# Two more tiles of each feed-forward stage by seven block products, and three of the four token sums on GpSimd, in a one-core macaron decoder layer

## The chip, the core and the metric

One Trainium2 chip, of which one core works. The metric is the device time of one execution of the whole layer in microseconds (us); three runs of the kernel before gave 2166.7, 2168.15 and 2168.75.

## What is computed

```python
x = x + 0.5 * _swiglu(_rmsnorm(x, ffn1_norm[l]), ffn1_w_gu[l], ffn1_w_down[l])
...
x = x + merged @ w_out[l]
x = x + 0.5 * _swiglu(_rmsnorm(x, ffn2_norm[l]), ffn2_w_gu[l], ffn2_w_down[l])

def _swiglu(h, w_gu, w_down):
    a, b = jnp.split(h @ w_gu, 2, axis=-1)
    return (jax.nn.silu(a) * b) @ w_down
```

1024 tokens, model width 1024, hidden width 2816, everything in float32. Between the two feed-forward stages stands a token-mixing block with three kinds of attention, which the change leaves alone. Each float32 product is made on TensorE from rounded parts: an operand is split into `hi` (rounded) and `lo` (the rest), and `hi*hi`, `hi*lo` and `lo*hi` are added up, so one product of blocks is three matmuls, and each operand needs an `hi` (made by ScalarE) and a `lo` (made by VectorE).

## The kernel before

**Layout.** Tokens lie transposed: `xT` holds 8 tiles of 128 model channels by 1024 tokens. The hidden width is 22 tiles of 128. A hidden tile needs a gate product and an up product (each 128 hidden by 1024 tokens, over 8 tiles of channels), then `silu(gate) * up / 2`, and two such tiles at a time (a group) are multiplied by their part of `w_down` and added to `xT`.

**Three ways to make a hidden tile.** Tiles 0 and 1 are made straight from `h = x * gain` (`h_hi`, `h_lo`), and scaled afterwards by the norm of each token (`rB`, in `ffn_gate`, `ffn_up`, lines 1427 to 1435). Each of these four products is a *unit* of 48 matmuls of 128x512. Tiles 2 and 3 (`by_halves`) are made with normed tokens instead, and are also 4 units of 48. From tile 4 on (`PLAIN = 4`) gate and up of one tile are made together as a product of 2x2 blocks by *seven* block products instead of eight; each block product is a *part* of 12 matmuls (`seventh`), so a tile is 84 matmuls instead of 96. From group 2 on the down product too is made by seven parts (`pair`).

**Normed tokens.** The seven products need the four quadrants of the normed tokens (512 channels by 512 tokens, stored as 128x2048) and four sums or differences of them. `quadrant` (L1454) makes one by four VectorE instructions from `xT`, gain and `rB`; `tokens_sum` (L1473) makes a sum; `tokens_hi` (L938, ScalarE) and `tokens_lo` (L1462, VectorE) split each into `tok_hi` and `tok_lo`, 128x2048 each. The buffers lie on top of `h_hi`, `h_lo` and of scratch memory.

**The order around the change.** Every engine runs a list written by hand and waits on semaphores. TensorE: gate and up of tiles 0 and 1; then `ffn`: the first half of the gate of tile 2 (24 matmuls), `down_plain` (group 0: eight output tiles `m`, 96 matmuls, first both `m = 0, 1` for hidden tile 0, then for hidden tile 1), the rest of tiles 2 and 3, then the parts of tiles 4 to 21. In the first stage a small product for the attention bias (`toe`) stands just ahead of `ffn`, and `down_plain` waits until VectorE has copied it out of PSUM (`toe_kept`), since it uses the same banks. VectorE scales and splits tiles 0 and 1, makes quadrants and `tok_lo`, adds each finished down tile to `xT` (`add_tile`, L1488), which also sets PSUM free for TensorE, and makes the `lo` of each part's weights (`part_lo`, L1581). GpSimd adds up squares for the norm (`square_sums`, L783) and makes the sums of weight blocks that the parts need (`weights_sum`, L804 to L812), in the order of its list.

The line on which TensorE waits in `down_plain` before it can go on to the second hidden tile:

```python
pe.wait_ge(split_done, u + 3)
pe.wait_ge(a_ready, A_COUNT * f + 2)
for m in range(2):
    whole(m, 1).then_inc(down_done, 1)
for m in range(2, DT):
    pe.wait_ge(down_added, ADD_COUNT * f + m - 1)
```

`a_ready` counts the finished `a_lo` (L1448) of hidden tiles 0 and 1, `f` is the stage (0 or 1).

Of the kernel before, what the change touches and what calls it, by code (L numbers as in the profile page):

```python
# [48 lines left out]

PLAIN, SEVEN, NQ = 4, 7, 4  # L50
TILES7 = FT - PLAIN
FFN_UNITS = 10
# [11 lines left out]
U_HALVES = (U_SB - 6, UNITS - 6)  # L64
# [83 lines left out]


# [188 lines left out]
def layer(nc, x, mem, weights, gains, head_gains, rel_bias, consts, onehot, out):  # L338
    ctx = ExitStack()
    with ctx:  # L340
# [42 lines left out]
        oh = at("oh", AR + 56 * K, [33, TOE])  # L383
# [3 lines left out]
        toe = at("toe", AR + 62 * K, [2, TOE])  # L387
# [27 lines left out]
        raw2 = [at("raw2_0", RAW, [P, 2, 1024]), at("raw2_1", WH + 4 * K, [P, 2, 1024])]  # L415
        RING = (WH, WL, WL + 4 * K, WL + 8 * K)
# [89 lines left out]
        mem_in, ident_in, cst_in, gain_in, hgain_in = (sem(n) for n in ("mem_in", "ident_in", "cst_in", "gain_in", "hgain_in"))  # L506
# [49 lines left out]
        tok_made, tok_hi_done, tok_split, a_summed = (sem(n) for n in ("tok_made", "tok_hi_done", "tok_split", "a_summed"))  # L556
# [12 lines left out]
        TILE_COUNT, TOK_COUNT = a_count(FT - 1), 22  # L569
# [22 lines left out]
        def after_slot(eng, f, n):  # L592

            if n >= NQ:
                eng.wait_ge(part_done, NPART * f + n - NQ + 1)
            else:
                eng.wait_ge(unit_done, U_HALVES[f] + (4, 4, 5, 6)[n])

        def after_chunk(eng, f, c, *halves):

            for half in halves:
                if c % 2:
                    eng.wait_ge(chunk_in[half], 16 * (CHUNKS // 2 * f + c // 2 + 1))
                else:
                    eng.wait_ge(raw_in[half], 16 * ((U_HALVES[f] + 6) // 2 + CHUNKS // 2 * f + c // 2 + 1))
# [115 lines left out]
        def _(sp):  # L721
# [10 lines left out]
            sp.dma_start(hg_raw[:], head_gains).then_inc(hgain_in, 16)  # L732
# [41 lines left out]
        def _(pool):  # L774
# [104 lines left out]
            square_sums(2)  # L879
            weights_sums(1)  # L880
# [3 lines left out]
        def _(act):  # L884
            def split_hi(k):
# [4 lines left out]
                if k in (U_SB, U_SB + 1):  # L890
# [37 lines left out]
            def tokens_hi(f, i):  # L928

                if i < 4:  # L930
                    act.wait_ge(tok_made, TOK_COUNT * f + 4 * i + 4)
                else:
                    act.wait_ge(tok_made, TOK_COUNT * f + 18 + (1, 3, 2, 4)[i - 4])
                if i == 4 and f == 0:
                    act.wait_ge(toe_out, 16)
                if i >= 6:
                    act.wait_ge(unit_done, U_HALVES[f] + 6)
                nc.scalar.activation(tok_hi[i][:], tok[i][:], ACT.Copy).then_inc(tok_hi_done, 1)  # L938

# [63 lines left out]
            def behind_part(f, n):  # L1003
# [6 lines left out]
                if p == 0:  # L1010
                    if t < PLAIN + 2:
                        act.wait_ge(unit_done, U_HALVES[f] + 2)
# [3 lines left out]
                elif p == 1:  # L1016
                    if i % TILES7:
                        act.wait_ge(glu_done, (TILE_COUNT - 2) * f + a_count(t - 1) - 3)
# [9 lines left out]
                elif t == FT - 1:  # L1028
                    act.wait_ge(glu_done, (TILE_COUNT - 2) * f + a_count(t) - 3)
                    act.wait_ge(part_done, NPART * f + part_at("pair", ND, 5) + 1)  # L1030
                    nc.scalar.activation(a_hi[s][:, T1], a_full[s][:, T1], ACT.Copy).then_inc(a_hi_done, 1)
                    act.wait_ge(glu_done, (TILE_COUNT - 2) * f + a_count(t) - 2)
                    nc.scalar.activation(a_hi[s][:, T0], a_full[s][:, T0], ACT.Copy).then_inc(a_hi_done, 1)

            def ffn(f):

                u = U_HALVES[f]
                split_hi(u + 2)
                tokens_hi(f, 2)
# [1946 lines left out]
```

## Time and profile before

| what | value |
|---|---|
| median of 3 runs | 2168.15 us |
| the profiled execution's own time | 2167.03 us |
| its span, first to last instruction | 2165.1 us |
| TensorE busy | 2146.0 us, 99% |
| VectorE busy | 1584.1 us, 73% |
| ScalarE busy | 911.7 us, 42% |
| GpSimd busy | 468.8 us, 22% |
| granted clock of TensorE | 1.0 |

The span is what the trace covers; the execution's own time is 1.9 us longer. Matmuls are pipelined, so that the duration of one (0.39 us) is longer than the step from one start to the next. PE is TensorE, PEld its weight loads, DVE VectorE, ACT ScalarE, POOL GpSimd, SP SyncE. "Idle before" in a row is the time in which the engine did nothing before it, with what ended that time.

### The profile page before, as it was taken

To read this page: it belongs to the slowest core of one execution; us is meant where nothing else is said; L and a number is where in the kernel's file an instruction comes from. 1 tells how busy PE (TensorE), PEld (TensorE's weight loads), DVE (VectorE), ACT (ScalarE), POOL (GpSimd) and SP (SyncE) were. 2 spreads that over 40 slices of the span, in tenths; PEclk is the share of its full clock that TensorE was granted. 3 is DMA by queue.
4 is the path that set the end of the run, shared out by engine and by line. 5 is a ranking of instruction groups with operands and counts; after the bars stand their busy time and mean duration, and the time that the engine had idled before them with its cause. 6 is when DMAs were issued, how large, how long until landed. Compare 5 with 4: busy or idle time off the path is not lost.

```text
span 2165.1 us, 26379 instructions
## 1 busy us (share of the span) xinstructions
PE 2146.0 (99%) x9968; PEld 1733.8 (80%) x9968; DVE 1584.1 (73%) x1809; ACT 911.7 (42%) x1433; POOL 468.8 (22%) x396
## 2 busy tenths in 40 slices
PE   8999999999999999999999999999999999999999
PEld 7788888888887777777778888888888888888887
DVE  7978888888888788777536343355778888888885
ACT  6334333443445777846443111133333344343433
POOL 3013333323333122221000000002013332333330
PEclk9999999999999999999999999999999999999999
DMA  5211111111113200011112111131111111111113
GB/s 174 63 59 59 50 58 59 59 47 42 59 59 105 88 30 20 20 49 40 40 21 78 49 49 52 56 127 39 49 49 59 59 59 42 47 59 59 54 54 98
DMA packets 47630, 126.55 MB, mean 58 GB/s; under 512 B 4301, under 2 KB 20973, under 8 KB 47248
## 3 DMA queue, kind: packets, MB, share of 16 engines
q1 hardware_dynamic: 45600, 112.61, 16.2%
q10 hardware_dynamic: 912, 10.11, 1.3%
q0 software_dynamic: 992, 2.15, 0.5%
q8 instruction: 80, 1.31, 0.3%
q14 instruction: 46, 0.38, 0.1%
HBM read 116.42 MB, written 9.87 MB: 58 GB/s over the span
## 4 chain that ended last, share of the span: by engine, by line
PE 92%; DVE 5%; issue 1%; ACT 1%; DMA 0%; POOL 0%; SPq 0%; DVEq 0%; ACTq 0%
PE ps L2153 91%; DVE h_lo L1410 1%; DVE tok_lo L1462 1%; PE ps L2770 0%; DVE xT L1755 0%; DVE q_lo L1581 0%; PE ps L2705 0%; DVE h_lo L2065 0%; DVE xT L1488 0%; PE ps L2865 0%; DVE w_lo L1403 0%; DMA x_nat<-in_x 0%; ACT sb_l L1212 0%; POOL sb_l L829 0%; DVE a_lo L1534 0%
## 5 line engine op out<-in xcount | busy, mean ns | idle before, releaser
L2153 PE MATMUL ps<-tok_hi,q_hi 128*128 128x512 f32 x1008 | 392.7, 390 | 1.4 <-issue 1.0
L2153 PE MATMUL ps<-tok_lo,q_hi 128*128 128x512 f32 x1008 | 392.2, 389 | 0.0
L2153 PE MATMUL ps<-tok_hi,q_lo 128*128 128x512 f32 x1008 | 392.1, 389 | 0.0
L2153 PE MATMUL ps<-h_hi,w_hi 128*128 128x512 f32 x960 | 373.2, 399 | 1.7 <-ACT h_hi L1135 1.1
L2153 PE MATMUL ps<-h_lo,w_hi 128*128 128x512 f32 x960 | 363.9, 391 | 2.6 <-DVE h_lo L1410 2.1
L1547 DVE TENSOR_TENSOR xT<-xT,ps 128x1024 f32<-128x1024 f32 x252 | 302.8, 1218 | 60.2 <-PE ps L2153 49.0
L2153 PE MATMUL ps<-h_hi,w_lo 128*128 128x512 f32 x960 | 305.4, 390 | 0.0
L2153 PEld LDWEIGHTS ps<-tok_hi,q_hi 128*128 128x128 f32 x1008 | 189.2, 188 | 42.7 <-issue 2.4
L2153 PEld LDWEIGHTS ps<-h_hi,w_hi 128*128 128x128 f32 x960 | 179.9, 188 | 51.3 <-issue 15.7
L2153 PEld LDWEIGHTS ps<-tok_hi,q_lo 128*128 128x128 f32 x1008 | 189.2, 188 | 39.3
L2153 PEld LDWEIGHTS ps<-tok_lo,q_hi 128*128 128x128 f32 x1008 | 189.3, 188 | 38.9
L2153 PEld LDWEIGHTS ps<-h_hi,w_lo 128*128 128x128 f32 x960 | 180.3, 188 | 38.7
L2153 PEld LDWEIGHTS ps<-h_lo,w_hi 128*128 128x128 f32 x960 | 180.1, 188 | 38.2 <-DVE h_lo L1410 2.5
L2153 PE MATMUL ps<-b_hi,q_hi 128*128 128x512 f32 x504 | 196.1, 389 | 0.0
L2153 PE MATMUL ps<-b_hi,q_lo 128*128 128x512 f32 x504 | 196.1, 389 | 0.0
L804 POOL TENSOR_TENSOR q_sum<-raw 128x512 f32<-128x512 f32 x72 | 78.7, 1093 | 526.9 <-PE ps L2153 366.6
L1403 DVE TENSOR_TENSOR w_lo<-raw,w_hi 128x1024 fp32r<-128x1024 f32 x84 | 115.1, 1373 | 76.8 <-ACT w_hi L896 67.4
L783 POOL TENSOR_TENSOR acc<-acc,sq 128x1024 f32<-128x1024 f32 x21 | 53.9, 2566 | 405.1 <-ACT sq L903 404.9
L2153 PE MATMUL ps<-a_lo,q_hi 128*128 128x512 f32 x352 | 137.0, 389 | 0.0
L1001 ACT ACTIVATE q_hi<-q_sum 128x512 fp32r<-128x512 f32 x108 | 68.3, 632 | 142.0 <-POOL q_sum L810 58.2
L2005 DVE TENSOR_TENSOR gate<-ps,rB 128x1024 f32<-128x1024 f32 x24 | 29.4, 1225 | 129.8 <-PE ps L2153 129.8
L1581 DVE TENSOR_TENSOR q_lo<-raw,q_hi 128x512 fp32r<-128x512 f32 x144 | 124.0, 861 | 0.0
(309 smaller groups left out, 3706.6 us busy)
## 6 DMA issues: line engine op xcount, KB each, us to landing
raw<-in_weights SPq DMA_DIRECT2D x195, 512.0 KB, 3.6
x_keep<-xT ACTq DMA_DIRECT2D x1, 4096.0 KB, 12.4
x_back<-x_keep ACTq DMA_DIRECT2D x1, 4096.0 KB, 12.2
x_nat<-in_x SPq DMA_DIRECT2D x7, 512.0 KB, 7.3
out<-y_nat SPq DMA_DIRECT2D x7, 512.0 KB, 3.2
toe_keep<-toe_row ACTq DMA_DIRECT2D x2, 704.0 KB, 6.2
m_nat<-in_mem SPq DMA_DIRECT2D x1, 1024.0 KB, 7.9
d_fB<-d_f_keep POOLq DMA_DIRECT2D x2, 512.0 KB, 6.3
```

The source lines that it names most:

```text
L783: nc.gpsimd.tensor_tensor(acc[:], acc[:], sq[:, k % 2, :], ALU.add).then_inc(acc_done, 1)
L804: nc.gpsimd.tensor_tensor(to, a21, a22, ALU.add).then_inc(w_summed, 1)
L1001: nc.scalar.activation(q_hi[n % NQ][:], src, ACT.Copy).then_inc(part_hi_done, 1)
L1403: nc.vector.tensor_tensor(w_lo[:, w_slot(k)].rearrange("p a b -> p (a b)"), raw[:, k % NRAW, :], w_hi[:, w_slot(k)].rearrange("p a b -> p ...
L1410: nc.vector.scalar_tensor_tensor(out=h_lo[:, k, :], in0=xT[:, k, :], scalar=g32[:, gain, k:k + 1], in1=h_hi[:, k, :].bitcast(F32), op0=ALU ...
L1462: nc.vector.tensor_tensor(tok_lo[i][:], tok[i][:], tok_hi[i][:].bitcast(F32), ALU.subtract).then_inc(tok_split, 1)
L1547: nc.vector.tensor_tensor(to, to, ps[:, 2 + half, :].rearrange("p (a c) -> p a c", a=2), ALU.add).then_inc(down_added, 1)
L1581: nc.vector.tensor_tensor(q_lo[n % NQ][:], src, hi, ALU.subtract).then_inc(part_split, 1)
L2005: nc.vector.tensor_tensor(gate_tile(m, b), ps[:, merge_pair(m, b), :], rB[:], ALU.mult).then_inc(mg_taken, 1)
L2153: return pe.matmul(o, a, b, start=start, stop=stop, skip_group_check=True)
```

## The change

Tiles 2 and 3 are made by seven block products too (`PLAIN = 2`); `by_halves`, `halves_silu` and `halves_product` go. Only 7 versions of the tokens are kept, instead of 8. Of the four sums VectorE makes one (`tok[1]`), inside the new `first_tokens`, and GpSimd three, in the new `tokens_sums`. VectorE makes all four quadrants ahead of scaling tile 1's up product, and all seven `tok_lo` between the additions of group 0. ScalarE makes all seven `tok_hi` only after the last plain gate or up unit (`unit_done >= U_END - GT`). Group 0's down tiles go over all four PSUM pairs (`first_pair`) instead of two. The weight slots become `k % 3`. The head gains' arrival is counted with the constants', and at the end of the first stage the split of the next unit's weights stands one part later.

```diff
-PLAIN, SEVEN, NQ = 4, 7, 4
+PLAIN, SEVEN, NQ = 2, 7, 4
...
+def first_pair(m):
+
+    return (2, 3, 0, 1, 2, 3, 2, 3)[m]
...
+            def tokens_sums(f):
+
+                pool.wait_ge(tok_made, TOK_COUNT * f + 13)
+                nc.gpsimd.tensor_tensor(tok[4][:], tok[3][:], tok[4][:], ALU.subtract).then_inc(tok_summed, 1)
+                pool.wait_ge(unit_done, U_END[f] - GT)
+                nc.gpsimd.tensor_tensor(tok[2][:], tok[3][:], tok[1][:], ALU.subtract).then_inc(tok_summed, 1)
+                pool.wait_ge(tok_made, TOK_COUNT * f + 17)
+                pool.wait_ge(tok_summed, TOK_SUMS * f + 2)
+                nc.gpsimd.tensor_tensor(tok[6][:], tok[5][:], tok[2][:], ALU.subtract).then_inc(tok_summed, 1)
+
             square_sums(0)
+            tokens_sums(0)
             weights_sums(0)
...
             def tokens_hi(f, i):
 
-                if i < 4:
-                    act.wait_ge(tok_made, TOK_COUNT * f + 4 * i + 4)
+                act.wait_ge(unit_done, U_END[f] - GT)
+                if i in (2, 4, 6):
+                    act.wait_ge(tok_summed, TOK_SUMS * f + {4: 1, 2: 2, 6: 3}[i])
...
+            def first_tokens(f):
+
+                quadrant(f, 4, 0, 1)
+                tokens_sum(f, 1, 4, 0, 8)
+
+            def other_tokens(f):
+
+                quadrant(f, 3, 1, 1)
+                quadrant(f, 5, 1, 0)
...
-                quadrant(f, 2, 0, 1)
                 add_tile(f, 0, 0)
+                tokens_lo(f, 0)
                 add_tile(f, 0, 1)
-                quadrant(f, 3, 1, 1, 0, 2)
+                tokens_lo(f, 1)
                 add_tile(f, 0, 2)
-                quadrant(f, 3, 1, 1, 2, 4)
+                tokens_lo(f, 2)
+                part_lo(f, 0)
                 add_tile(f, 0, 3)
-                tokens_lo(f, 2)
-                add_tile(f, 0, 4)
                 tokens_lo(f, 3)
...
+                part_lo(f, 1)
+                for i in range(4, SEVEN):
+                    add_tile(f, 0, i)
+                    tokens_lo(f, i)
+                add_tile(f, 0, DT - 1)
...
                 for m in range(2, DT):
-                    pe.wait_ge(down_added, ADD_COUNT * f + m - 1)
+                    if m == 2:
+                        pe.wait_ge(gate_scaled, GT * (f + 1))
+                    elif m == 3:
+                        pe.wait_ge(up_scaled, PLAIN * (f + 1))
+                    else:
+                        pe.wait_ge(down_added, begin + (1, 2, 5, 6)[m - 4])
...
-                u = U_HALVES[f]
-                pe.wait_ge(split_done, u + 1)
-                pe.wait_ge(gate_scaled, 2 * f + 2)
-                by_halves(f, 0, u, 0)
                 down_plain(f)
-                by_halves(f, 0, u, 1).then_inc(unit_done, 1)
...
-                by_halves(f, 1, u + 5, 0)
-                by_halves(f, 1, u + 5, 1).then_inc(unit_done, 1)
                 for n in range(NPART):
                     pe.wait_ge(part_split, NPART * f + n + 1)
```

VectorE's list in the second feed-forward stage, around the end of tile 1's up product. Before (`tok_113` to `tok_120` are the eight token buffers in order, `a_up_80` the scaled up product of tile 1, `a_lo_76` the piece that TensorE waits for, L1488 the additions to `xT`):

```order
L1454 SCALAR_TENSOR_TENSOR tok_114<-xT,g_58,rB 128x512 x4
L1462 TENSOR_TENSOR tok_lo_106<-tok_114,tok_hi_98 128x2048
L1435 SCALAR_TENSOR_TENSOR a_up_80<-ps,rB 128x1024
L1442 TENSOR_TENSOR a_full_72<-a_up_80,a_full_72 128x1024
L1444 CAST a_hi_82<-a_full_72 128x1024
L1403 TENSOR_TENSOR w_lo<-raw,w_hi 128x1024
L1448 TENSOR_TENSOR a_lo_76<-a_full_72,a_hi_82 128x1024
L1454 SCALAR_TENSOR_TENSOR tok_115<-xT,g_58,rB 128x512 x4
L1488 TENSOR_TENSOR xT<-xT,ps 128x1024 x2
```

With the change (`tok_111` to `tok_117` are the seven buffers, `tok_104` and up their `lo`; L1446 is `quadrant`, L1461 `tokens_sum`, L1427 and L1434 to L1440 scale and split tile 1):

```order
L1446 SCALAR_TENSOR_TENSOR tok_115<-xT,g_58,rB 128x512 x4
L1461 TENSOR_TENSOR tok_112<-tok_115,tok_111 128x2048
L1422 TENSOR_TENSOR a_full_72<-ps,rB 128x1024
L1395 TENSOR_TENSOR w_lo<-raw,w_hi 128x1024
L1446 SCALAR_TENSOR_TENSOR tok_114<-xT,g_58,rB 128x512 x4
L1446 SCALAR_TENSOR_TENSOR tok_116<-xT,g_58,rB 128x512 x4
L1427 SCALAR_TENSOR_TENSOR a_up_80<-ps,rB 128x1024
L1434 TENSOR_TENSOR a_full_72<-a_up_80,a_full_72 128x1024
L1436 CAST a_hi_82<-a_full_72 128x1024
L1440 TENSOR_TENSOR a_lo_76<-a_full_72,a_hi_82 128x1024
```

Between the gate scaling (L1422) and the up scaling (L1427) of tile 1 stood one quadrant, and now two stand; a sum stands ahead of the gate scaling. The `tok_lo` and the `w_lo` of tile 2's weights are gone from this place.

What follows on VectorE with the change, from the first addition (L1486 is `add_tile`, L1456 `tokens_lo`, L1572 `part_lo`); the pattern goes on to the eighth addition:

```order
L1486 TENSOR_TENSOR xT<-xT,ps 128x1024
L1456 TENSOR_TENSOR tok_lo_104<-tok_111,tok_hi_97 128x2048
L1486 TENSOR_TENSOR xT<-xT,ps 128x1024
L1456 TENSOR_TENSOR tok_lo_105<-tok_112,tok_hi_98 128x2048
L1486 TENSOR_TENSOR xT<-xT,ps 128x1024
L1456 TENSOR_TENSOR tok_lo_106<-tok_113,tok_hi_99 128x2048
L1572 TENSOR_TENSOR q_lo_124<-raw_0_118,q_hi_120 128x512
L1486 TENSOR_TENSOR xT<-xT,ps 128x1024
L1456 TENSOR_TENSOR tok_lo_107<-tok_114,tok_hi_100 128x2048
L1572 TENSOR_TENSOR q_lo_125<-q_sum_129,q_hi_121 128x512
L1486 TENSOR_TENSOR xT<-xT,ps 128x1024
```

Before, two `tok_lo` and two quadrants stood between the eight additions; now it is seven `tok_lo` and two `part_lo`.

GpSimd's list with the change, where before the first weight sum (`q_sum<-raw`) followed directly on the sums of squares:

```order
L784 TENSOR_TENSOR acc<-acc,sq 128x1024 x7
L824 TENSOR_TENSOR tok_115<-tok_114,tok_115 128x2048
L826 TENSOR_TENSOR tok_113<-tok_114,tok_112 128x2048
L829 TENSOR_TENSOR tok_117<-tok_116,tok_113 128x2048
L805 TENSOR_TENSOR q_sum_129<-raw_0_118 128x512
L808 TENSOR_TENSOR raw_0_118<-q_sum_129,raw_0_118 128x512
```

Three instructions of 128x2048 have come in between, each with both inputs in SBUF.

## Rows read from the trace of the kernel before

**Rows 1.** Page, busy time of each engine, share of the span and instructions
```profile
PE 2146.0 (99%) x9968; PEld 1733.8 (80%) x9968; DVE 1584.1 (73%) x1809; ACT 911.7 (42%) x1433; POOL 468.8 (22%) x396
```
**Rows 2.** Waits of TensorE over the span: total us, times, longest us
```profile
PE ps L2153 <- DVE h_lo L1410: 2.1, 1, 2.1
PE ps L2153 <- issue: 1.0, 2, 0.5
PE ps L2153 <- DVE q_lo L1581: 0.4, 2, 0.2
```
**Rows 3.** Timeline, TensorE, second stage: start us, us, instruction, count
```profile
1549.88 0.39 PE L2153 MATMUL ps<-tok_hi,w_hi 128*128 128x512 f32 x1
...
1555.32 0.39 PE L2153 MATMUL ps<-a_hi,w_hi 128*128 128x512 f32 x1
...
1615.73 0.39 PE L2153 MATMUL ps<-tok_hi,q_hi 128*128 128x512 f32 x1
```
**Rows 4.** Timeline, VectorE, second stage, around the end of tile 1's up product
```profile
1540.04 1.22 DVE L1430 TENSOR_TENSOR a_full<-ps,rB 128x1024 f32<-128x1024 f32 x1
1543.33 1.23 DVE L1403 TENSOR_TENSOR w_lo<-raw,w_hi 128x1024 fp32r<-128x1024 f32 x1 [2.07 <-ACT w_hi L896]
1544.47 2.73 DVE L1454 SCALAR_TENSOR_TENSOR tok<-xT,g,rB 128x512 f32<-128x512 f32 x4
...
1551.40 1.22 DVE L1435 SCALAR_TENSOR_TENSOR a_up<-ps,rB 128x1024 f32<-128x1024 f32 x1
1552.72 1.23 DVE L1442 TENSOR_TENSOR a_full<-a_up,a_full 128x1024 f32<-128x1024 f32 x1
1553.98 0.69 DVE L1444 CAST a_hi<-a_full 128x1024 fp32r<-128x1024 f32 x1
...
1555.73 1.22 DVE L1448 TENSOR_TENSOR a_lo<-a_full,a_hi 128x1024 fp32r<-128x1024 f32 x1
```
**Rows 5.** Timelines of GpSimd and VectorE at 18 us and at 1508 us
```profile
18.70 2.39 POOL L783 TENSOR_TENSOR acc<-acc,sq 128x1024 f32<-128x1024 f32 x1 [1.07 <-ACT sq L903]
...
19.77 2.40 DVE L1410 SCALAR_TENSOR_TENSOR h_lo<-xT,g,h_hi 128x1024 fp32r<-128x1024 f32 x1
...
1507.68 5.81 DVE L1410 SCALAR_TENSOR_TENSOR h_lo<-xT,g,h_hi 128x1024 fp32r<-128x1024 f32 x3
...
1508.93 3.47 POOL L783 TENSOR_TENSOR acc<-acc,sq 128x1024 f32<-128x1024 f32 x1 [9.37 <-ACT sq L903]
```
**Rows 6.** Timelines of VectorE (input in PSUM) and GpSimd at 126 us
```profile
126.04 1.23 DVE L1504 SCALAR_TENSOR_TENSOR a_full<-ps,a_full 128x1024 f32<-128x1024 f32 x1 [0.80 <-PE ps L2153]
...
126.09 1.29 POOL L804 TENSOR_TENSOR q_sum<-raw 128x512 f32<-128x512 f32 x1 [85.47 <-PE ps L2153]
```
**Rows 7.** Groups by line: busy us, mean ns; and durations, min/median/max ns
```profile
L1488 DVE TENSOR_TENSOR xT<-xT,ps 128x1024 f32<-128x1024 f32 x31 | 37.8, 1218 | 21.3 <-PE ps L2153 20.6
L1462 DVE TENSOR_TENSOR tok_lo<-tok,tok_hi x16: 2282/2285/3380, 72.8 to 1624.3; 128x2048 fp32r<-128x2048 f32 x16
L938 ACT ACTIVATE tok_hi<-tok x16: 1898/1920/1922, 64.1 to 1620.9; 128x2048 fp32r<-128x2048 f32 x16
```
**Rows 8.** Timelines of VectorE and TensorE in the first stage
```profile
72.76 2.28 DVE L1462 TENSOR_TENSOR tok_lo<-tok,tok_hi 128x2048 fp32r<-128x2048 f32 x1
...
79.14 2.53 PE L2153 MATMUL ps<-oh,rel 33*2 33x256 f32 x10
...
83.02 1.20 DVE L1819 COPY toe<-ps 2x1024 f32<-2x1024 f32 x1
84.15 0.54 DVE L1820 COPY toe<-ps 2x384 f32<-2x384 f32 x1
...
137.28 0.68 DVE L1581 TENSOR_TENSOR q_lo<-raw,q_hi 128x512 fp32r<-128x512 f32 x1
```
**Rows 9.** Timeline, TensorE, opening: eight transposes after idle time, and later
```profile
9.85 1.91 PE L2477 MATMUL ps<-cst,x_nat 128*128 128x128 f32 x8
...
15.16 1.03 PE L2477 MATMUL ps<-cst,x_nat 128*128 128x128 f32 x8
```

More of the change, by code:

```diff
@@ L96 @@
     CHUNK += [("tile", _t)]
-    if _t % 2 == 1:
+    if _t % 2 == 1 and _t > 3:
         CHUNK += [("pair", (_t - 3) // 2)]
@@ L100 @@
         PARTS += [("tile", _t, _p, _c)]
-        if _t % 2 == 1:
+        if _t % 2 == 1 and _t > 3:
             PARTS += [("pair", (_t - 3) // 2, _p, _c + 1)]
@@ L1668, in ffn @@
                         pair_sums(f, (of - 2) // 2, p == 2)
-                    if kind == "tile" and of % 2 == 0 and p >= 2:
+                    if kind == "tile" and of % 2 == 0 and of > PLAIN and p >= 2:
                         pair_lo(f, (of - 2) // 2, p - 2)
-                    if kind == "tile" and of % 2 == 1 and p == 0:
+                    if kind == "tile" and of % 2 == 1 and of > PLAIN + 1 and p == 0:
                         pair_lo(f, (of - 3) // 2, 5)
@@ L1678, in ffn @@
                     if kind == "down":
-                        if f == 0 and n == NPART - 2:
+                        if f == 0 and n == NPART - 1:
                             split_lo(U_SB)
@@ L1800, in _ @@
             ffn_up(0, U_FIRST[0][1], 0)
-            quadrant(0, 0, 1, 0)
+            quadrant(0, 0, 0, 0)
             proj_final(1)
@@ L1811, in _ @@
             proj_final(3)
-            tokens_lo(0, 0)
+            first_tokens(0)
+            split_lo(9)
             dve.wait_ge(unit_done, U_MEM[3] + 1)
-            quadrant(0, 1, 0, 0)
-            split_lo(9)
-            tokens_lo(0, 1)
+            other_tokens(0)
             ffn_up(0, U_FIRST[1][1], 1)
@@ L2134, in _ @@
             ffn_gate(1, U_FFN2, 0)
+            quadrant(1, 0, 0, 0)
             split_lo(U_FFN2 + 3)
-            quadrant(1, 0, 1, 0)
             ffn_up(1, U_FFN2 + 1, 0)
@@ L2139, in _ @@
             split_lo(U_FFN2 + 4)
-            tokens_lo(1, 0)
+            first_tokens(1)
             ffn_gate(1, U_FFN2 + 2, 1)
             split_lo(U_FFN2 + 5)
-            quadrant(1, 1, 0, 0)
-            tokens_lo(1, 1)
+            other_tokens(1)
             ffn_up(1, U_FFN2 + 3, 1)
-            glu_product(1, 1, lambda: split_lo(U_FFN2 + 6))
+            glu_product(1, 1)
             ffn(1)
@@ L2226, in gate_or_up_part @@
                     last.then_inc(unit_done, 1)
-            def by_halves(f, part, k, half):
-                for half_d in (1, 0):
-                    i = ((1, 0), (2, 3))[half][half_d]
-                    pe.wait_ge(tok_split, 8 * f + i + 1)
-                    for j in range(4):
-                        hi, lo = (w[:, w_slot(k), 4 * half_d + j, :] for w in (w_hi, w_lo))
-                        mm(bank(2 * part + half), hi, tok_hi[i][:, j, :], half_d == 1 and j == 0, False)
-                        mm(bank(2 * part + half), hi, tok_lo[i][:, j, :], False, False)
-                        last = mm(bank(2 * part + half), lo, tok_hi[i][:, j, :], False, half_d == 0 and j == 3)
-                return last
             def seventh(f, n):
@@ L2258, in seventh @@
                     pe.wait_ge(seven_added, 3 * i + 2)
-                pe.wait_ge(tok_split, 8 * f + (5, 5, 6, 6, 7, 7, 8)[p])
+                pe.wait_ge(tok_split, SEVEN * f + p + 1)
                 for j in range(4):
                     hi, lo = (w[n % NQ][:, j * P:(j + 1) * P] for w in (q_hi, q_lo))
-                    mm(to, hi, tok_hi[of][:, j, :], j == 0 and p in (0, 1, 5), False)
-                    mm(to, hi, tok_lo[of][:, j, :], False, False)
-                    last = mm(to, lo, tok_hi[of][:, j, :], False, j == 3)
+                    mm(to, hi, tok_hi[p][:, j, :], j == 0 and p in (0, 1, 5), False)
+                    mm(to, hi, tok_lo[p][:, j, :], False, False)
+                    last = mm(to, lo, tok_hi[p][:, j, :], False, j == 3)
                 last.then_inc(part_done, 1)
@@ L2935, in pair @@
         return [two[:, :D], two[:, D:]]
-    plain = tile(0) + tile(1) + tile(2)[:1] + down(0) + tile(2)[1:] + tile(3)
+    plain = tile(0) + tile(1) + down(0)
     chunks = [unit for kind, of in CHUNK for unit in (seven(of) if kind == "tile" else pair(of))]
```

207 lines of the change are left out of this document (73 added, 134 removed).

## The prediction

> **What bounds the kernel now.** The page comes first: TensorE is busy for 2146 of 2165 us, VectorE for 73%, GpSimd for 22% [rows 1]. Then the waits of TensorE, which say whether that 99% is work or queueing: the longest inside the layer is 2.1 us, and around the feed-forward joins there are only two of 0.5 us and two of 0.2 us [rows 2]. So time is matmuls times their step, and any new wait of TensorE counts in full. The step comes from the timeline [rows 3]: 24 matmuls stand between 1549.88 and 1555.32, that is 5.44 us, or 0.2267 us each.
>
> **What goes.** Per stage two tiles of 96 matmuls become two of 84, so 2 x 2 x 12 = 48 matmuls in all: 48 x 0.2267 = **-10.9 us**. TensorE's own gaps in the stretch that is rewritten go too. From 1549.88 to the first part at 1615.73 [rows 3] are 65.85 us, and the work there is 4 x 48 + 96 = 288 matmuls, 65.28 us: 0.6 us, and about the same in the first stage: **-1.3 us** for both.
>
> **What comes: cover is lost and the port is shared.** Before, 24 matmuls (5.44 us) on tokens stood between tile 1's up product and the down product [rows 3], and 120 more behind it hid the sums and `tok_lo`. Now the down product starts at once: TensorE has 12 matmuls (2.7 us) until it needs `a_lo` of tile 1, and after the down product the first part needs the tokens.
>
> How do GpSimd's sums share with VectorE? Two places tell. At 18.70 GpSimd adds for 2.39 us, and an `h_lo` (both inputs in SBUF) that starts at 19.77 takes 2.40 us, though it takes about 1.2 alone: it got nearly nothing until GpSimd ended at 21.09. At 1508.93 GpSimd takes 3.47 instead of 2.39: it waits 1.07 us for the running `h_lo`, and then three of these take 5.81 us together instead of 3.5 [rows 5]. So they take turns by whole instructions, and a waiting one gets the next turn. An instruction whose input is in PSUM is not in this: 1.23 us beside GpSimd's 1.29 [rows 6]. The Trainium skill, "SBUF — State Buffer", section "Who interferes with whom", says the same as an exclusive lock for the whole instruction; the trace agrees (2.40 for 1.2 us).
>
> A GpSimd sum of 128x2048 is in no row. From 1.29 us for 512 columns and 2.39 for 1024 [rows 5, 6] a further 512 cost 1.10, so I take 2.39 + 2 x 1.10 = 4.6 us. Bounds: 5.2, four times the 512-wide one, and 4.4, should a wider instruction be a little cheaper per column than these two lengths say. The Trainium skill, "GPSIMD Engine Reference", section 3.1, gives 4497 ns for it against 2293 on VectorE; by that the sum would be some 0.6 us less. VectorE's steps are the durations less some 0.08 us by which neighbours overlap: additions 1.13, `tok_lo` 2.20 [rows 7], a quadrant 2.66, `w_lo` 1.14 [rows 4], a part's `lo` 0.6 [rows 8].
>
> *Second stage, until `a_lo`.* The gate is scaled at 1539.6 to 1540.8, ScalarE makes silu and `w_hi`, and `w_lo` ends at 1544.2, much as before [rows 4], since all of it waits for TensorE's gate product. Quadrant 3 ends at 1546.4, and that lets GpSimd go. From here they take turns: first piece of quadrant 5 to 1546.9; **sum 4** to 1551.5; second piece; **sum 2** (up product long done) 1552.0 to 1556.6; the last pieces to 1557.7. **Sum 6** runs 1557.7 to 1562.3, beside the scaling from PSUM, but the product `a_up * a_full` needs the port: 1562.3 to 1563.4; GpSimd's first weight sum 1.3 us; the cast to 1565.2; the second weight sum; `a_lo` to 1567.5. Before it ended at 1556.95 [rows 4]. TensorE is through its 12 matmuls at 1549.88 + 2.72 = 1552.6: it waits **14.9 us**.
>
> *Second stage, the additions.* Let A be the end of `a_lo`. The first down tile is out at A + 1.6. The down tile `m = 6` needs the fifth addition. Until then VectorE does five additions, four `tok_lo` and two part splits: 5 x 1.13 + 4 x 2.20 + 2 x 0.6 = 15.7, so A + 17.2; TensorE alone would be there at A + 60 x 0.2267 = A + 13.6: it waits **3.6 us**. Then `tok_lo` 4 and addition 5 (3.33 us) against 2.72: **0.6 us**. After that each part (2.72 us) finds its tokens ready. Sum 19.2 us. ScalarE's seven `tok_hi` (1.83 each) start after the up product, the third behind the first weight sum, and stay about 3 us ahead; the weight transfers have the whole wait to land. I cost both at nothing.
>
> *First stage.* VectorE comes to `first_tokens` at 72.8 [rows 8] and is busy from there: quadrant, sum, `w_lo`, quadrant are 2.66 + 2.2 + 1.1 + 2.66 = 8.7, so 81.2 with the first piece; sum 4 to 85.8, sum 2 86.3 to 90.9, rest of the quadrant 92.0, scaling 93.1, the two bias copies 94.7. TensorE is through the bias product at 81.6 (79.14 + 2.46, ten matmuls) and now waits for these copies: **13.1 us** (before, they were made at 83.0 to 84.7 beside the token matmuls [rows 8]). Sum 6 holds the port to 96.6; product, weight sum, cast, weight sum, `a_lo` end at 101.8 against 97.5: **4.4 us**; then 3.6 and 0.6 as above. Sum 21.8 us.
>
> *Slow matmuls after the waits.* Eight transposes took 1.91 us behind the idle opening and 1.03 later [rows 9], so TensorE comes back at half speed. Two matmul groups at half speed delay the first addition by 1.36 us, per stage: **+2.7**. Later matmuls have slack against VectorE. Bounds 0, and 3 us a stage if the second pause cools it too. The Trainium skill, "TensorE: Matmul & The Clock Gate", Part 1, gives the same two levels, 1.2 GHz behind idle time and 2.4 GHz when busy.
>
> **Edits at nothing.** The head gains are issued right behind the constants at the start, and VectorE is busy until it needs them. The split of the next unit one part later at the end of stage one: VectorE's list there is as long as before, and TensorE waits for its end anyway (2.1 us for `h_lo` [rows 2]); 0, bounds -1 and +1. Slots and buffer places: nothing.
>
> **Sum.** -10.9 - 1.3 + 19.2 + 21.8 + 2.7 = **+31.5 us**. The profiled execution took 2167.0, so 2198.5; the median of the runs lies 1.1 above it: **2199.7 us**. With the bounds of the GpSimd sum (each 0.1 us of it moves a stage by 0.3) and of the slow matmuls: 2195 to 2209.
>
> **Rivals.**
> - *The port costs nothing* (turns taken only in part, or sums much shorter). For: 22% of GpSimd, most sums hidden today. Against: rows 5. Then the waits are lost cover alone: in stage two 2.1 us (`a_lo` at 1554.7 against 1552.6), then 4.6 (the third `tok_lo` comes 1 us late, since its buffer is read by sum 6) and 0.6, so 7.3; in stage one 4.8 for the copies, 0.4, 3.8 and 0.6, so 9.6. With 1.3 for slow matmuls, 16.9 + 1.3 - 12.2 = +6.0: 2174 us.
> - *Faster.* One mechanism: VectorE's list is not late at the join, so TensorE finds each addition made and only `a_lo` is waited for. The change wins if the waits of a stage stay under 12.2 / 2 = 6.1 us. With 2.1 and 5.2 us alone: -12.2 + 7.3 = -4.9: 2163.2 us. Against it stand the 15.7 us of VectorE work for 13.6 us of matmuls, which no turn-taking enters.
> - *Worse.* VectorE loses more turns (weight sums between the `tok_lo`, too) and TensorE runs at half speed after each pause: some 8 us more, 2208 us.
> - *The change doesn't do what it says*: the matmuls in the two programs differ by 48 of 128x512, as said, so no chance is given.
>
> **How the numbers follow.** Forecast (turns by whole instructions) 0.84, worse 0.05, port free 0.08, faster 0.03. A difference of 0.2% (4.3 us) is about what a measurement tells from none. Faster by more: 0.02, most of the faster case. Within: 0.02, the rest of it and the near side of the port-free case. Slower: 0.96. The forecast and the worse case lie in 2188 to 2209: below it are left the port-free case and the faster one, and its lower end allows for about a third of the port waits to be missed.
>
> **What would show it.** TensorE's waits: one of about 15 us in stage two and of 13 and 4 us in stage one, for `a_lo` and the bias copies, then 3.6 us for an addition. GpSimd: three instructions of 4.6 us per stage, and quadrant pieces of 5 us beside them. The port-free case would show sums of 4.6 us beside `tok` pieces of 0.75. The prediction is wrong if TensorE's waits in each stage are under 10 us, or if they lie elsewhere, say at the parts (late weight chunks).

## The result, and the profile after

The changed kernel takes **2203.9 us** (median of 4 runs, 2202.1 to 2205.6) against 2167.4 for the kernel before on the same chip: ratio 1.0168, 95% interval 1.0156 to 1.0180. It is 36.5 us slower; the forecast was 31.5 slower and 2199.7, its range 2188 to 2209.

The page of the changed kernel, busy time of each engine and the granted clock in 40 slices (answers to [rows 1]):

```profile
PE 2142.7 (97%) x9920; PEld 1730.3 (79%) x9920; DVE 1611.0 (73%) x1833; ACT 924.7 (42%) x1467; POOL 519.9 (24%) x418
...
PEclk9899999999999999999999999999899999999999
```

The 48 matmuls are gone, TensorE is busy only 3.3 us less, and at both joins a slice of the clock falls to 8. Where TensorE waits (us in total, times, longest; answers to [rows 2]):

```profile
PE ps L2124 <- DVE a_lo L1440: 17.4, 2, 16.0
PE ps L2124 <- DVE toe L1792: 13.9, 1, 13.9
PE ps L2124 <- DVE xT L1486: 7.1, 3, 3.7
...
PE ps L2124 <- DVE w_lo L1395: 3.6, 2, 2.5
```

The first three are the forecast waits. The fourth was not forecast. The timelines of GpSimd and VectorE in the second stage (start us, us, instruction; answers to [rows 4]):

```profile
1563.80 1.23 DVE L1395 TENSOR_TENSOR w_lo<-raw,w_hi 128x1024 fp32r<-128x1024 f32 x1 [2.08 <-ACT w_hi L911]
1564.94 14.00 DVE L1446 SCALAR_TENSOR_TENSOR tok<-xT,g,rB 128x512 f32<-128x512 f32 x8
1578.86 1.21 DVE L1427 SCALAR_TENSOR_TENSOR a_up<-ps,rB 128x1024 f32<-128x1024 f32 x1
1580.18 4.42 DVE L1434 TENSOR_TENSOR a_full<-a_up,a_full 128x1024 f32<-128x1024 f32 x1
1584.63 1.63 DVE L1436 CAST a_hi<-a_full 128x1024 fp32r<-128x1024 f32 x1
1586.30 2.17 DVE L1440 TENSOR_TENSOR a_lo<-a_full,a_hi 128x1024 fp32r<-128x1024 f32 x1
...
1567.75 5.06 POOL L824 TENSOR_TENSOR tok<-tok,tok 128x2048 f32<-128x2048 f32 x1 [31.91 <-DVE tok L1446]
1572.77 4.96 POOL L826 TENSOR_TENSOR tok<-tok,tok 128x2048 f32<-128x2048 f32 x1
1579.02 4.50 POOL L829 TENSOR_TENSOR tok<-tok,tok 128x2048 f32<-128x2048 f32 x1 [1.29 <-DVE tok L1446]
```

Eight quadrant pieces take 14.00 us, where [rows 4] have 2.73 for four; the product takes 4.42 instead of 1.23 and ends 1.1 us behind GpSimd's third sum. A scaling whose input is in PSUM takes its usual 1.21 beside that sum. TensorE at the joins, with its idle time (answers to [rows 3]):

```profile
95.19 0.77 PE L2124 MATMUL ps<-a_hi,w_hi 128*128 128x512 f32 x1 [13.93 <-DVE toe L1792]
...
102.07 0.47 PE L2124 MATMUL ps<-a_hi,w_hi 128*128 128x512 f32 x1 [1.42 <-DVE a_lo L1440]
...
119.61 0.79 PE L2124 MATMUL ps<-a_hi,w_hi 128*128 128x512 f32 x1 [3.66 <-DVE xT L1486]
...
127.62 0.39 PE L2124 MATMUL ps<-tok_hi,q_hi 128*128 128x512 f32 x1
...
1569.74 0.39 PE L2124 MATMUL ps<-a_hi,w_hi 128*128 128x512 f32 x1
...
1588.62 0.77 PE L2124 MATMUL ps<-a_hi,w_hi 128*128 128x512 f32 x1 [16.00 <-DVE a_lo L1440]
...
1607.43 0.50 PE L2124 MATMUL ps<-a_hi,w_hi 128*128 128x512 f32 x1 [3.13 <-DVE xT L1486]
...
1613.64 0.39 PE L2124 MATMUL ps<-tok_hi,q_hi 128*128 128x512 f32 x1
```

A first matmul of 0.77 to 0.80 us is one at half speed (1.2 GHz); the next ones then follow at 0.43 us instead of 0.2267. A pause costs some 0.3 us more than the idle time in its row: that time starts at the recorded end of the matmul before (0.39 us long, of which a step is only 0.2267), and the first step after a pause at full speed is 0.34 us. At the end of stage one stands one more half-speed stretch, eight matmuls long, behind the wait for `w_lo`:

```profile
704.57 0.84 PE L2124 MATMUL ps<-h_hi,w_hi 128*128 128x512 f32 x2 [2.54 <-DVE w_lo L1395]
705.21 1.05 PE L2124 MATMUL ps<-h_hi,w_lo 128*128 128x512 f32 x2
```

**The ledger.** From the end of tile 1's up product to the first part, stage two took 65.85 us before [rows 3] and takes 43.90 now (1569.74 to 1613.64). 168 matmuls (38.09 us) moved from this stretch into parts, so the like-for-like change is **+16.1 us** (forecast 14.5). The same from the bias product on: before 79.14 [rows 8] to 147.60, 68.5 us; now 78.73 to 127.62, 48.9 + 38.1: **+18.5** (forecast 17.1). The end of stage one: `w_lo` 3.6 us in place of `h_lo` 2.1 [rows 2], **+1.5**, and **+1.7** for the half-speed stretch behind it, which the kernel before doesn't have (forecast 0 for both). The rest, -3.0, is what is left to 34.8, the change of the two spans: 0.4 of it comes ahead of the bias product, and some 1.2 in each stage are the gaps of the first parts [rows 2], with what each costs beyond its row, that are gone (from the first part to the end stage two took 549.4 us before, and takes 548.2 now without the 38.09 that moved there); 0.2 is not placed. The medians differ by 36.5, 1.7 more than the two profiled spans.

### The profile page after: what moved, and what is told of

It is laid out like the page before. It is cut to its first block, busy times and chain, and to the rows that moved or that the text cites. A ratio compares the mean times of both kernels' runs of the same rounds, so it can differ in the third digit from the quotient of the medians.

```text
span 2199.9 us, 26498 instructions
## 1 busy us (share of the span) xinstructions
PE 2142.7 (97%) x9920; PEld 1730.3 (79%) x9920; DVE 1611.0 (73%) x1833; ACT 924.7 (42%) x1467; POOL 519.9 (24%) x418
## 4 chain that ended last, share of the span: by engine, by line
PE 88%; DVE 8%; issue 1%; ACT 1%; DMA 0%; POOL 0%; SPq 0%; DVEq 0%; ACTq 0%
PE ps L2124 87%; DVE tok L1446 2%; DVE h_lo L1402 1%; DVE w_lo L1395 1%; DVE xT L1486 1%; DVE tok_lo L1456 0%; PE ps L2717 0%; DVE a_full L1434 0%; DVE xT L1729 0%; PE ps L2652 0%; DVE h_lo L2037 0%; PE ps L2812 0%; DMA x_nat<-in_x 0%; DVE a_lo L1440 0%; ACT w_hi L911 0%
## 5 line engine op out<-in xcount | busy, mean ns | idle before, releaser
L2124 PE MATMUL ps<-tok_hi,q_hi 128*128 128x512 f32 x1120 | 435.8, 389 | 0.0
L2124 PE MATMUL ps<-tok_lo,q_hi 128*128 128x512 f32 x1120 | 435.7, 389 | 0.0
L2124 PE MATMUL ps<-tok_hi,q_lo 128*128 128x512 f32 x1120 | 435.7, 389 | 0.0
L2124 PEld LDWEIGHTS ps<-tok_hi,q_hi 128*128 128x128 f32 x1120 | 210.3, 188 | 43.9 <-DVE q_lo L1572 0.3
L2124 PEld LDWEIGHTS ps<-tok_hi,q_lo 128*128 128x128 f32 x1120 | 210.3, 188 | 43.6
L2124 PEld LDWEIGHTS ps<-tok_lo,q_hi 128*128 128x128 f32 x1120 | 210.3, 188 | 43.5
L805 POOL TENSOR_TENSOR q_sum<-raw 128x512 f32<-128x512 f32 x76 | 86.3, 1136 | 398.7 <-PE ps L2124 239.0
L1395 DVE TENSOR_TENSOR w_lo<-raw,w_hi 128x1024 fp32r<-128x1024 f32 x76 | 108.8, 1432 | 72.8 <-ACT w_hi L911 62.2
L1008 ACT ACTIVATE q_hi<-q_sum 128x512 fp32r<-128x512 f32 x120 | 75.9, 633 | 175.3 <-POOL q_sum L811 65.9
L1572 DVE TENSOR_TENSOR q_lo<-raw,q_hi 128x512 fp32r<-128x512 f32 x160 | 140.3, 877 | 2.9 <-ACT q_hi L1008 2.9
L813 POOL TENSOR_TENSOR q_sum<-raw 128x512 f32<-128x512 f32 x76 | 88.6, 1166 | 179.2 <-PE ps L2124 179.2
```

What stands on the lines that cost most here:

```text
L805: nc.gpsimd.tensor_tensor(to, a21, a22, ALU.add).then_inc(w_summed, 1)
L813: nc.gpsimd.tensor_tensor(to, a22, a21, ALU.subtract).then_inc(w_summed, 1)
L1008: nc.scalar.activation(q_hi[n % NQ][:], src, ACT.Copy).then_inc(part_hi_done, 1)
L1395: nc.vector.tensor_tensor(w_lo[:, w_slot(k)].rearrange("p a b -> p (a b)"), raw[:, k % NRAW, :], w_hi[:, w_slot(k)].rearrange("p a b -> p ...
L1572: nc.vector.tensor_tensor(q_lo[n % NQ][:], src, hi, ALU.subtract).then_inc(part_split, 1)
L2124: return pe.matmul(o, a, b, start=start, stop=stop, skip_group_check=True)
```

## The experiments

Theory: a GpSimd sum of 4.6 us holds the shared SBUF port, VectorE's chain to `a_lo` stands behind three of them, and the lost cover lets TensorE feel it. Rivals: lost cover alone (the sums cost VectorE nothing); a list that is late wherever the sums stand. All times are compared with 2203.9 for the changed kernel and 2167 to 2168 for the one before, which ran beside each; the changed kernel did not run beside them, so a difference of a microsecond or two from it says little.

### narrow_sums: the sums at a quarter of their width

```diff
-nc.gpsimd.tensor_tensor(tok[4][:], tok[3][:], tok[4][:], ALU.subtract)
+nc.gpsimd.tensor_tensor(tok[4][:, 0, :], tok[3][:, 0, :], tok[4][:, 0, :], ALU.subtract)
...
```

> GpSimd's three sums of normed tokens cover 512 columns of each row instead of 2048 (left out: the other three quarters of these sums; the tokens of products 2 and 6 are filled from what is there). All waits between the engines stay. Turns at the port (my theory): a sum takes 1.3 instead of 4.6 us, so in stage two the quadrants end about 5 us sooner, the product waits for no long sum, and TensorE's wait for a_lo falls from 16.0 to some 7 us; in stage one the wait for the bias copies falls from 13.9 to 8 and the one for a_lo goes. The waits for additions stay near 3 us. Together about 16 us less than the changed kernel: 2187 us (2182 to 2194). Lost cover alone (the sums cost VectorE nothing): no change from 2203.9, and the waits for a_lo and the copies stay at 16 and 14 us.

Measured **2184.3 us** (2183.5 to 2184.4), 19.6 less. TensorE's waits:

```profile
PE ps L2129 <- DVE toe L1797: 7.5, 1, 7.5
PE ps L2129 <- DVE xT L1491: 7.2, 3, 3.7
PE ps L2129 <- DVE a_lo L1444: 6.4, 1, 6.4
```

The chain's waits shrink as forecast (16.0 to 6.4; 13.9 to 7.5; the 1.4 gone) and those for additions stay. The chain to `a_lo` and to the bias copies waits for none of these sums, so their length reaches it only through the turns. It is worth 19.6 us.

### vector_sums: the same sums on VectorE

```diff
 quadrant(f, 3, 1, 1)
+late_sum(f, 0)
 quadrant(f, 5, 1, 0)
+late_sum(f, 1)
+late_sum(f, 2)
```

> The changed kernel with the three sums on VectorE, each right behind the quadrants that it needs, and nothing else moved. Turns at the port: a sum of 4.6 us on GpSimd blocks VectorE for all of it, and on VectorE it costs 2.2 us, so VectorE gets more work and the chain still gets shorter: in stage two a_lo comes 4 to 5 us sooner (TensorE's wait 11 instead of 16.0), in stage one the wait for the bias copies stays at about 14 and the one for a_lo goes. 2198 us (2195 to 2201), some 6 less than the changed kernel. If GpSimd's sums cost VectorE nothing, this edit adds 6.6 us to its list in each stage, and the kernel gets slower: 2217 us.

Measured **2196.1 us** (2195.4 to 2197.9), 7.8 less: VectorE does 13 us more of its own work (six sums of 2.2) and the kernel gets faster. This is the run that lost cover alone can't explain, since by it the sign would be the other one. TensorE's waits:

```profile
PE ps L2131 <- DVE toe L1799: 14.4, 1, 14.4
PE ps L2131 <- DVE a_lo L1434: 11.3, 1, 11.3
```

### late_sums: GpSimd's sums behind `a_lo`

```diff
+pool.wait_ge(a_ready, A_COUNT * f + 2)
 pool.wait_ge(tok_made, TOK_COUNT * f + 13)
```

> The three sums are whole, but GpSimd starts them only when a_lo of tile 1 is there. Turns at the port: the first waits shrink (a_lo in stage two from 16.0 to about 2 us, bias copies in stage one from 13.9 to 5), and the cost comes back one step later: each tok_lo now waits for a sum of 4.6 us in turn, VectorE reaches the fifth addition about 15 us late, and TensorE waits for xT there. Time 2203 us (2196 to 2209), hardly moved. Lost cover alone: once the sums stand behind the chain nothing is blocked, and the kernel comes to 2174 us (up to 2180).

Measured **2200.7 us** (2199.3 to 2201.5). The waits moved as expected (`toe` 5.4, `a_lo` 2.3, then 14.4 and 14.2 for `xT`). But how the second wait comes about is not as expected. GpSimd and ScalarE in stage two:

```profile
1579.98 6.66 POOL L827 TENSOR_TENSOR tok<-tok,tok 128x2048 f32<-128x2048 f32 x1
1586.79 6.59 POOL L830 TENSOR_TENSOR tok<-tok,tok 128x2048 f32<-128x2048 f32 x1
1593.34 1.26 POOL L805 TENSOR_TENSOR q_sum<-raw 128x512 f32<-128x512 f32 x1
...
1594.70 0.63 ACT L1009 ACTIVATE q_hi<-q_sum 128x512 fp32r<-128x512 f32 x1 [19.93 <-POOL q_sum L805]
1595.24 9.09 ACT L953 ACTIVATE tok_hi<-tok 128x2048 fp32r<-128x2048 f32 x5
```

Two sums take 6.6 us, that is 4.5 and a turn of VectorE's `tok_lo`, so about 4 of the 14 us of the new wait are turns. The rest is GpSimd's own queue: ScalarE's next `tok_hi` stands behind a `q_hi` that waits for a weight sum, and that is behind the three sums. Such a wait would come without any port too, so the 2174 us given for lost cover alone was put too low, and this run does not tell the two apart; the two above do.

### rotate and rotate_spread: the wait for additions

```diff
 def first_pair(m):
-    return (2, 3, 0, 1, 2, 3, 2, 3)[m]
+    return m % 4
...
-if f == 0:
-    pe.wait_ge(toe_kept, 2)
 for m in range(2):
-    after(pe, down_added, begin + m - 1)
+    if m == 0:
+        pe.wait_ge(gate_scaled, GT * (f + 1))
+    else:
+        pe.wait_ge(up_scaled, PLAIN * (f + 1))
     whole(m, 0)
...
```

The rotation moves waits too: the second down tile (`m = 1`) now lies in the banks of tile 1's up product and waits for its scaling (`a_up`), and the bias copies are waited for only ahead of `m = 2`.

> The changed kernel, with the down product of the first two tiles going round all four pairs of PSUM banks (0, 1, 2, 3, 0, 1, 2, 3) instead of 2, 3, 0, 1, 2, 3, 2, 3, so that a down tile needs the addition of four tiles before, not of two. My account: TensorE's waits for xT (3.66 in stage one, 3.13 + 0.32 in stage two) go, and with the one in stage one the half-speed stretch behind it (2.5 us): 9.6 us less, 2194.3 us (2192 to 2197). Rival: the wait only moves to the first part, since VectorE's list (additions and tok_lo) is as long as before: 2.5 to 4 us less, 2200 us or more.

Measured **2202.1 us** (2201.8 to 2202.7), 1.8 less, hardly outside the scatter of the changed kernel (2202.1 to 2205.6), and not the 9.6 of my account: the rival was right. TensorE's waits:

```profile
PE ps L2124 <- DVE a_up L1427: 19.5, 2, 10.7
PE ps L2124 <- DVE a_lo L1440: 11.2, 2, 5.6
PE ps L2124 <- DVE q_lo L1572: 6.5, 2, 3.3
```

The waits for `xT` are gone and 3.3 and 3.2 us for the `lo` part of the third part's weights are new: it stood behind all additions and all seven `tok_lo`. Also, the pause before `a_lo` is now cut in two, and TensorE came back at half speed from both; and behind the 3.3 us pause of stage one it fell to half speed from the fourth matmul on, for 1.7 us. The next run mends the list:

```diff
-for i in range(4, SEVEN):
-    add_tile(f, 0, i)
-    tokens_lo(f, i)
-add_tile(f, 0, DT - 1)
+add_tile(f, 0, 4)
+add_tile(f, 0, 5)
+tokens_lo(f, 4)
...
+for i in {0: (5,), 1: (6,)}.get(n, ()):
+    tokens_lo(f, i)
+if n in (0, 1):
+    add_tile(f, 0, 6 + (0, 1).index(n))
```

> The rotation over four pairs of banks again, and VectorE's list mended where the wait went: the lo parts of weights for the third and fourth part no longer stand behind all additions and all seven tok_lo, but between them (tok_lo 5 and 6 and the additions 6 and 7 go into the first two parts). GpSimd's sums stay as they are. If the wait for q_lo of the third part (3.33 and 3.21 us in the rotated kernel) came from the order of the list alone, it goes, and nothing takes its place: 6.5 us under the rotated kernel's 2202.1, so 2195.6 us (2194 to 2199). If VectorE's sum of work is what is late, the wait moves to a later part and the time stays over 2199 us.

Measured **2195.8 us** (2195.4 to 2196.3): the `q_lo` wait goes and only 1.0 us ("issue") takes its place in stage two. That half-speed stretch is gone with the wait. The late additions were list order, not work.

### narrow_spread: do the two add up?

> rotate_spread with GpSimd's three sums at 512 of 2048 columns (left out: the other three quarters of them, as in narrow_sums). It asks whether turns at the port and the late additions are separate costs: narrow sums alone took 19.6 us off the changed kernel, rotation and spread list alone 8.1. If they add up: 2176 us (2173 to 2179). If both shorten the same wait, it stays above 2181.

Measured **2177.0 us** (2176.3 to 2177.8). 19.6 and 8.1 apart, 26.9 together: the port turns and the order of the list are separate costs. With both taken away the kernel is still 9 us slower than before. That is what lost cover costs here over the 12.2 us saved, with the remaining short turns, half-speed stretches and `w_lo` waits in it.

### split_first: the wait that was not forecast

```diff
+if f == 0 and n == NPART - 1:
+    split_lo(U_SB)
 if n:
     behind_part(f, n - 1, finish)
...
-if f == 0 and n == NPART - 1:
-    split_lo(U_SB)
```

> The changed kernel with one line moved: the lo part of the first weights of the next stage (at the end of stage one) is made ahead of the addition and gain of the part before, not behind them. TensorE waited 2.54 us for it at 704.6 (and 1.0 us for the next one). If its place in VectorE's list is the cause, the 2.54 us go and some 1 to 2 us come back as a wait for h_lo behind it: 2202 us (2201 to 2203.5), 1 to 2 less. If the cause is the port (a turn of GpSimd's sums of squares held this instruction for 2.2 of its 3.4 us), it only changes places: no change.

Measured **2203.2 us** (2200.7 to 2204.4): no change. Both `w_lo` waits (3.6 us) went and one of 2.6 for `h_lo` came, 1 us less; but in its profiled execution TensorE came back from a shorter pause in stage two at half speed, where the changed kernel did not:

```profile
1607.06 0.79 PE L2124 MATMUL ps<-a_hi,w_hi 128*128 128x512 f32 x1 [2.79 <-DVE xT L1486]
```

So the place in the list moves the wait; no run puts the split back into the part where it stood before, and whether the port or the amount of work there holds the rest was not tried.

### chain_first, spread_list, copy_first, adds_last: a version that beats both?

All four put the sums on VectorE, rotate the bank pairs, and put scaling, product and `a_lo` of tile 1 ahead of both late quadrants and of the bias copies in stage one, and ahead of the last quadrant in stage two:

```diff
-other_tokens(0)
 ffn_up(0, U_FIRST[1][1], 1)
+glu_product(0, 1)
 dve.wait_ge(toe_done, 1)
...
-glu_product(0, 1)
...
-other_tokens(1)
+quadrant(1, 3, 1, 1)
+late_sum(1, 0)
 ffn_up(1, U_FFN2 + 3, 1)
```

> A version meant to beat both: the sums are made by VectorE (2.2 us each instead of 4.6 of GpSimd in turn), scaling, product and a_lo of tile 1 come ahead of the quadrants and of the bias copies, the four-pair rotation as in the run beside it, and the split of the next weights at the end of stage one stands ahead of the last additions. By the same account TensorE waits about 2 us in stage two and 0 to 5 us in stage one (its parts wait some 1 to 2 us each for tok_lo). Against 12.2 us of work and gaps saved this gives 2161 us (2155 to 2170), under the kernel before (2167.4). If lost cover and turns are not the cause, it stays above 2180.

Measured **2192.2 us** (2191.0 to 2192.7), 31 more than expected. The joins were as computed (0.5 us for `a_lo` in stage one, 2.7 in stage two), but the fault of `rotate` was built in again:

```profile
PE ps L2138 <- DVE q_lo L1576: 27.8, 3, 13.2
```

`spread_list` spreads the list, lets ScalarE copy the bias, and holds the weight sums until `a_lo`:

```diff
-nc.vector.tensor_copy(toe[:, 0:1024], ps[0:2, 2, :]).then_inc(toe_kept, 1)
+nc.scalar.activation(toe[:, 0:1024], ps[0:2, 2, :], ACT.Copy).then_inc(toe_kept, 1)
...
 if n + 2 < NPART:
     part_lo(f, n + 2)
+if n == 0 and f == 0:
+    late_sum(f, 0)
+if n < 4:
+    tokens_lo(f, n + 3)
+if n in (1, 3):
+    add_tile(f, 0, 6 + n // 2)
```

> The version chain_first, whose waits were 13.15 and 12.68 us for q_lo of the third part at the end of VectorE's list. Here the list is spread: tok_lo 3 to 6, the last additions and (in stage one) sum 4 stand between the lo parts of weights of the first four parts; the bias copies are made by ScalarE; GpSimd's weight sums wait for a_lo. By the sum of VectorE's steps the parts of stage one wait 4 to 5 us in all, stage two 2.5 us for a_lo and 0 to 1 in the parts. With 12.2 us less work: 2163 us (2158 to 2170), level with or a little under the kernel before (2167.2). If the sevenths need more VectorE work than TensorE covers however it is ordered, it stays above 2175.

Measured **2180.7 us** (2179.8 to 2181.2). One wait made the difference, and it was on ScalarE: the copy that frees a bank stood behind three `tok_hi`, of which the first waited for sum 4:

```profile
114.60 5.51 ACT L946 ACTIVATE tok_hi<-tok 128x2048 fp32r<-128x2048 f32 x3 [10.60 <-DVE tok L1475]
120.02 0.61 ACT L1002 ACTIVATE q_hi<-q_sum 128x512 fp32r<-128x512 f32 x1
120.54 0.57 ACT L1016 ACTIVATE a_full<-ps 128x512 f32<-128x512 f32 x1
...
121.21 0.77 PE L2138 MATMUL ps<-tok_hi,q_hi 128*128 128x512 f32 x1 [11.80 <-ACT a_full L1016]
```

`copy_first` moves `tok_hi` 4 to 6 behind the copies of the first parts (`if n in (1, 2, 3): tokens_hi(f, n + 3)` in ScalarE's loop), and holds GpSimd's weight sums until `a_lo` in stage two only:

> spread_list with the fault of its ScalarE list mended: there the copy of the first part out of PSUM stood behind a tok_hi that waited for sum 4, and TensorE waited 11.80 us for that copy in stage one (1.74 in stage two). Now tok_hi 4 to 6 come behind the copies of the first parts, and in stage one GpSimd's weight sums are free to start early again. What is left is VectorE's list: by its steps the parts of stage one wait some 6 to 7 us in all, those of stage two 2 to 3 us behind 1.7 us for a_lo. 2171 us (2168 to 2176), 9 less than spread_list and still 4 over the kernel before, whose 12.2 us of extra TensorE work and gaps would then be no dearer than the waits. Rival: the waits left come from single places in the lists and go too: 2163 us or less.

Measured **2176.0 us** (2174.8 to 2177.9), at the upper end: six waits for `q_lo`, 12.1 us in all. Last, the two additions that nobody needs yet go into the last two of tile 2's seven parts:

```diff
-if n in (1, 3):
-    add_tile(f, 0, 6 + n // 2)
+if n in (5, 6):
+    add_tile(f, 0, n + 1)
```

> copy_first (2176.0) waited 12.1 us in six waits for q_lo, and VectorE stood without a gap from the scaling on. Here the additions 6 and 7 of the first down product, whose bank pairs nobody needs before the first pair of tiles, move from the second and fourth part into the sixth and seventh. If VectorE's list is what is late, each stage gets 1.1 to 2.3 us back: 2172 us (2169.5 to 2174.5), 4 less than copy_first and still about 4 over the kernel before. If the parts waited for their own weights (GpSimd's weight sums and ScalarE's q_hi, not for VectorE's turn to come), nothing changes: 2176 us.

Measured **2169.0 us** (2167.6 to 2170.2) against 2167.8 before: ratio 1.0007, interval 0.9998 to 1.0016, no difference. The gain of 7 is more than the 4 expected: the waits for `q_lo` are 4.1 us less, the one for `a_lo` 0.5 less, and where `copy_first` had two half-speed stretches at the join of stage one (behind pauses of 2.11 and 2.58 us, 3.4 us lost) there is one (behind 2.93 us, 2.0 lost). VectorE from 79 to 132 us, first in the kernel before, then here (stretch, its length, busy time and instructions, granted clock, DMA share, GB/s):

```profile
79.00:132.00 53.00, 46.80 (x36) 1.00 0.15 50
```
```profile
79.00:132.00 53.00, 52.65 (x42) 0.97 0.16 50
```

VectorE is full for 53 us. Five waits for `q_lo` (8.0 us) and 1.7 for `a_lo` are left, and the 12.2 us of TensorE's work and gaps are paid back nearly whole. No version was found that beats the kernel before.

## Why the prediction was right

**What goes** (-12.2): as forecast; 9920 instead of 9968 matmuls. The gaps of the first parts, some 2.4 us, went too, which the sum didn't have. They nearly cancel the 3.2 us at the end of stage one, which it didn't have either, and that is luck.

**Size of a sum** (4.6 us): 4.50 us undisturbed at 1579.02. The others take 5.06 and 4.96, which is 4.5 and the rest of the piece that VectorE had running. The Trainium skill, "GPSIMD Engine Reference", section 3.1, had 4497 ns; the trace agrees.

**Turns by whole instructions.** Shown by the order in stage two (sum, piece, sum, pieces, sum, product) and by `narrow_sums` and `vector_sums`. The Trainium skill's exclusive lock ("SBUF — State Buffer", "Who interferes with whom") is what these rows look like; that the waiting engine gets the next turn is from the rows.

**Stage two until `a_lo`** (14.9): 16.0. Counted from the end of the up product, the first sum ended 1.4 us later than I had it and `a_lo` 1.1 later; between them each sum was 0.1 shorter than my 4.6, and the other steps were right. 1.0 of the 1.4 is the gate scaling: I had it 10.3 us ahead of the end of the up product, the trace before has 9.8 [rows 3, 4], and now, behind `first_tokens` with its added sum, it is 9.2; silu, `w_hi` and `w_lo` follow it. The other 0.4 is a slip in the working: `w_lo` at 1544.2 and a quadrant of 2.66 give 1546.9 and not 1546.4. "Much as before" was the failing word.

**Stage one** (13.1 and 4.4): 13.9 and 1.4. The second is smaller only because the twelve matmuls ahead of it ran at half speed and took 5.5 us instead of 2.7: 4.1 together.

**Additions** (3.6 + 0.6 in each stage): 3.66 and 0, 3.13 and 0.32.

**Slow matmuls** (+2.7 for both): the term that was sized too low. In stage two nine ran at half speed and cost 1.9 us, where I had 1.36 for six. With the 0.3 us that each of three pauses costs beyond its row, which I had at nothing, that is 2.7 (43.90 less 96 matmuls, 21.76, less 19.45 of waits). In stage one the first twelve hid in the wait behind them, but the pause of 3.66 us cooled it once more, for another 2.5: the bound that I had named ("if the second pause cools it too"). The pause at the end of stage one added 1.7. So half speed cost 6.1 us beyond the waits, where the sum has 2.7.

**Edits at nothing.** The split of the next unit was priced at -1 to +1 and cost +1.5: TensorE waited 2.5 and 1.0 us for `w_lo` in place of 2.1 for `h_lo`, and the half-speed stretch behind it cost 1.7 more. Why `w_lo` is late there stays open.

**Rivals.** Port free (2174): fell with `vector_sums`. But without the long sums and with a mended list the kernel stands at 2177, near it. Faster (2163): the chain_first series shows why not: even with every wait at the join but 2 us gone, VectorE's list is too long. Worse (2208): part of it is real, the half speed, which followed four of the pauses.

## What to carry to other kernels

Work given to GpSimd is not free for VectorE when both read SBUF: price it at the whole length of the GpSimd instruction for whatever VectorE has next with its inputs in SBUF (a scaling from PSUM was not held: 1.21 us). Here 2.2 us on VectorE were cheaper than 4.5 beside it. Before work is taken from the engine that is 99% busy, add up what its neighbour must do in the shorter stretch; when a wait is removed, look what stands behind it in the same list, since four of these runs only moved it. An operation that frees a bank should never stand behind one that waits for something else.

## What the hardware showed that was not expected

Whether TensorE comes back at half speed does not follow from the length of the pause alone. It did after 3.66 us (stage one), after 2.79 (`split_first`, stage two), after 2.11 (`copy_first`) and after 2.54 (the changed kernel, end of stage one), and did not after 3.13 (the changed kernel, the same place as the 2.79, the same instructions) or 3.21 (`rotate`, stage two). It then ran some 6 to 13 matmuls of 128x512 at 0.43 us each, 1.4 to 2.8 us lost. The fall can also come after the restart: behind the pause of 3.33 us in `rotate`, stage one, three matmuls ran at full speed and the next eight at half (1.7 us lost), and so it was behind 2.93 us in `adds_last`.

```profile
131.59 0.50 PE L2124 MATMUL ps<-tok_hi,q_hi 128*128 128x512 f32 x1 [3.33 <-DVE q_lo L1572]
131.93 0.40 PE L2124 MATMUL ps<-tok_lo,q_hi 128*128 128x512 f32 x1
...
132.41 0.63 PE L2124 MATMUL ps<-tok_hi,q_hi 128*128 128x512 f32 x1
132.84 0.63 PE L2124 MATMUL ps<-tok_lo,q_hi 128*128 128x512 f32 x1
```

The granted clock in the changed kernel's stage two: half through the long pause and after it, full through the short one.

```profile
1580.00:1584.00 4.00, 0.00 (x0) 0.50 0.00 0
...
1588.00:1592.00 4.00, 3.38 (x8) 0.50 0.00 0
1592.00:1596.00 4.00, 4.00 (x18) 0.94 0.00 0
...
1604.00:1608.00 4.00, 0.87 (x5) 1.00 0.00 0
```
